# Router and step-size products with the thin weights stationary, in four column quarters of TensorE

## The reference

```python
g_prob = jax.nn.softmax((t @ w_rg + b_rg).astype(f32), axis=-1)      # 4 groups
e_logits = (t @ w_re + b_re).astype(f32).reshape(-1, N_GROUPS, EXPERTS_PER_GROUP)   # 16 experts
```

```python
dt = jax.nn.softplus((dt_raw + dt_bias).astype(jnp.float32))
log_f = jax.nn.log_sigmoid((f_raw + forget_b).astype(jnp.float32))
```

## Time and profile before

| | |
|---|---|
| median of 3 runs | 1540.35 us (1536.69 to 1540.72) |
| profiled execution | 1541.78 us, its span 1539.9 us |
| TensorE busy | 1384.1 us, 90% of the span |
| TensorE weight loads | 735.5 us, 48% |
| VectorE, ScalarE, GpSimd | 443.7, 240.1, 100.9 us |
| read from HBM | 355.14 MB, 231 GB/s over the span |
| mean granted clock of TensorE | 0.948 |
| L2045 (three routers), busy | 19.6 us, 96 passes |
| L2513 (step sizes), busy | 7.0 us, 32 passes |

### The profile page before, as it was taken

One profiled execution on the slowest core, in us unless ns is written; L12 is line 12 of the kernel. 1 busy time (PEld: TensorE's weight loads), 2 busy tenths in 40 slices (PEclk: granted clock), 3 DMA queues, 4 the chain that ended last, 5 costly groups with the idle time before them and its releaser, 6 DMA issues.

```text
span 1539.9 us, 18825 instructions
## 1 busy us (share of the span) xinstructions
PE 1384.1 (90%) x7765; PEld 735.5 (48%) x7765; DVE 443.7 (29%) x1252; ACT 240.1 (16%) x591; POOL 100.9 (7%) x190
## 2 busy tenths in 40 slices
PE   3999898999898888989997999979998699998996
PEld 3446554444445555554444874554455433333332
DVE  1104443221303355332214252251113721001113
ACT  0004210111101254101111222011320112010000
POOL 1110000000111000000001000000000011222210
PEclk9999989999998699989998899979999699999998
DMA  8957835999843356429999343365338147999990
GB/s 323 354 148 279 264 110 199 367 344 349 293 145 109 127 203 191 152 105 338 341 341 351 113 161 109 110 224 186 109 110 325 57 169 278 381 387 387 385 333 28
DMA packets 214687, 357.41 MB, mean 232 GB/s; under 512 B 15830, under 2 KB 85903, under 8 KB 214603
## 3 DMA queue, kind: packets, MB, share of 16 engines
q1 hardware_dynamic: 201314, 352.50, 64.6%
q10 hardware_dynamic: 13289, 3.71, 1.1%
HBM read 355.14 MB, written 1.05 MB: 231 GB/s over the span
## 4 chain that ended last, share of the span: by engine, by line
PE 82%; DVE 8%; DMA 4%; issue 3%; ACT 2%; SPq 1%; POOL 0%; DVEq 0%; ACTq 0%; POOLq 0%
PE bank L1924 19%; PE bank L2086 7%; PE bank L2284 6%; PE bank L2112 4%; PE bank L2127 4%; PE bank L2524 4%; PE bank L2144 4%; PE bank L2014 4%; PE bank L1939 3%; PE bank L2346 3%; DMA ring<-in_w_down 3%; PE bank L2571 3%; PE bank L2252 2%; PE bank L2377 2%; PE bank L2294 2%
## 5 line engine op out<-in xcount | busy, mean ns | idle before, releaser
L1924 PE MATMUL bank<-ring,hT 128*128 128x512 f32 x416 | 182.7, 601 | 3.2 <-ACT hT L804 3.0
L1924 PEld LDWEIGHTS bank<-ring,hT 128*128 128x128 f32 x416 | 79.9, 193 | 103.3 <-issue 99.9
L2086 PE MATMUL bank<-ring,A 128*64 128x512 f32 x512 | 113.4, 595 | 6.2 <-issue 3.2
L1924 PE MATMUL bank<-ring,OT 128*128 128x512 f32 x256 | 112.4, 600 | 3.0 <-issue 1.7
L1939 PE MATMUL bank<-ring,cact 128*32 128x128 f32 x2304 | 83.0, 298 | 24.5 <-DMA ring<-in_ada_w 14.7
L2284 PE MATMUL bank<-ring,A 128*64 128x512 f32 x384 | 86.9, 594 | 0.6 <-DMA ring<-in_w_up 0.6
L1939 PEld LDWEIGHTS bank<-ring,cact 128*32 128x32 f32 x2304 | 68.1, 119 | 36.8 <-issue 25.2
L682 POOL TENSOR_TENSOR rstd<-rstd,nhalf 128x1 f32<-128x1 f32 x20 | 17.2, 858 | 981.8 <-DVE rstd L1148 981.8
L1924 PEld LDWEIGHTS bank<-ring,OT 128*128 128x128 f32 x256 | 49.0, 193 | 64.2 <-issue 61.5
L2112 PE MATMUL bank<-pb 128*128 128x128 f32 (+1 forms) x512 | 64.4, 279 | 7.7 <-DVE A L1365 5.4
L2086 PEld LDWEIGHTS bank<-ring,A 128*64 128x64 f32 x512 | 36.2, 137 | 72.0 <-issue 68.7
(11 more groups left out here) (429 smaller groups left out, 1698.2 us busy)
## 6 DMA issues: line engine op xcount, KB each, us to landing
ring<-in_ada_w SPq DMA_DIRECT2D x24, 2048.0 KB, 8.7
ring<-in_moe_w_gate SPq DMA_DIRECT2D x32, 1024.0 KB, 7.2
ring<-in_moe_w_up SPq DMA_DIRECT2D x32, 1024.0 KB, 10.1
ring<-in_moe_w_down SPq DMA_DIRECT2D x16, 2048.0 KB, 12.9
ring<-in_w_gate SPq DMA_DIRECT2D x16, 2048.0 KB, 13.6
ring<-in_w_up SPq DMA_DIRECT2D x16, 2048.0 KB, 13.7
ring<-in_w_down SPq DMA_DIRECT2D x16, 2048.0 KB, 20.5
ring<-in_w_in SPq DMA_DIRECT2D x13, 2048.0 KB, 12.2
```

The costliest lines, as they stand in the source:

```text
L1924: ins = mm(B[2 * (m % 2) + tt][:], lhs[:, c, tt * P:(tt + 1) * P], w[:, c, :], start=c == 0, stop=c == C - 1)
L2086: ins = mm(B[4][n * b:n * (b + 1), :], h3[:, c, n * b:n * (b + 1)], wv[b][:, :, c, :], start=c == 0, stop=c == C - 1)
```

## The change

Three routers and the step-size product are computed the other way round. The thin weights (20 or 24 columns of a chunk) become the stationary operand and the 128 tokens of `hT` are streamed. Chunk c goes to the column quarter c % 4: its result of 20 or 24 rows stands at the partitions 32 * q of `B[2]`, and the eight chunks add up in pairs there. A product of zeros with 256 streamed columns clears the bank first. ScalarE copies the 128 x 256 of `B[2]` to `thin` in SBUF (`thin_copied`). Two products with that copy as stationary operand and a 128 x 24 matrix `fold` (ones where row 32 * q + j meets column j) add up the four quarters and turn the tokens back to the partitions, into the same place in `B[7]` or `B[6]` as before.

The order changes too. Token tile 0's products stand right behind `gate_spread` and ahead of tile 1's transposes; tile 1's, the copy and the fold stand where the router stood. For the step sizes both tiles' products stand where the old products did, and the fold comes after the first tile of `xbc`, with the signal for VectorE. GpSimd makes `fold` at the start with a memset and four selects. In two places on VectorE a wait for an own semaphore becomes `step`, a wait of the same kind.

The third MoE's work by halves of the experts is in the kernel before already; the diff holds nothing of it.

```diff
--- before.py
+++ after.py
@@ -247,6 +247,12 @@
         return ap.unsqueeze(axis).broadcast_to(shape)
 
 
+    fold = cols[:, 320:344]
+    thin = PT[:].rearrange("p a b -> p (a b)")[:, 0:T]
+    THIN = {"h1": 0, "h3": 1, "h4": 2, "h5": 3}
+
     def trans_evacuated(eng, k):
 
         eng.wait_ge(s["tr_act"] if k % 2 == 0 else s["tr_dve"], k // 2 + 1)
@@ -623,7 +629,11 @@
             pool.wait_ge(s["pool_step"], steps[0])
 
         g = nc.gpsimd
+        g.memset(fold, 0.0)
         step(g.memset(ident[:], 0.0))
+        for q in range(4):
+            step(g.affine_select(out=fold, in_=fold, compare_op=ALU.not_equal, fill=1.0, base=-32 * q,
+                                 pattern=[[-1, 24]], channel_multiplier=1))
         step(g.affine_select(out=ident[:], in_=ident[:], compare_op=ALU.not_equal, fill=1.0, base=0,
                              pattern=[[-1, P]], channel_multiplier=1))
         g.memset(zeros[:], 0.0)
@@ -774,6 +784,11 @@
                 if k % 2 == 0:
                     act.wait_ge(s["tr_ready"], k + 1)
                     op(k - TRANS[name], B[4]).then_inc(s["tr_act"], 1)
+
+        def thin_copied(hname):
+
+            act.wait_ge(s["thin_made"], THIN[hname] + 1)
+            a.copy(thin, B[2][:, 0:T]).then_inc(s["thin_out"], 1)
 
         def mod_out(G):
 
@@ -988,6 +1003,7 @@
         trans_out("h1", modulated(0, 3), [0])
         gate_rows(1)
         trans_out("h1", modulated(0, 3), [1])
+        thin_copied("h1")
         routing_exp(act, "moe0")
         moe_act("moe0")
         mod_out(3)
@@ -1022,10 +1038,12 @@
         act.wait_ge(s["proj_dve"], PROJ_DVE[PROJ["odout"] + 1])
         act.dma_start(rowp[:, 0, :], p["final_g"].partition_broadcast(P)).then_inc(s["rows_param"], 16)
         trans_out("h3", modulated(1, 3), [1])
+        thin_copied("h3")
         routing_exp(act, "moe1")
         moe_act("moe1")
         mod_out(6)
         trans_out("h4", modulated(2, 0))
+        thin_copied("h4")
 
         act.wait_ge(s["dt_abs"], 1)
         a.activation(dts[:, 1], dts[:, 1], ACT.Exp).then_inc(s["dt_exp"], 1)
@@ -1088,6 +1106,7 @@
         trans_out("h5", modulated(2, 3), [0])
         gate_rows(5)
         trans_out("h5", modulated(2, 3), [1])
+        thin_copied("h5")
         act.wait_ge(s["ln_scaled"], 1)
         routing_exp(act, "moe2")
         wide_act()
@@ -1346,9 +1365,8 @@
             step(v.tensor_tensor(rt[:, :, 4, :], rt[:, :, 4, :], rt[:, :, 7, 2:3].broadcast_to([P, TT, 4]), ALU.mult))
             step(v.tensor_tensor(rt[:, :, 5, :], rt[:, :, 5, :], rt[:, :, 7, 3:4].broadcast_to([P, TT, 4]), ALU.mult))
             step(v.tensor_tensor(rt[:, :, 4, :], rt[:, :, 4, :], rt[:, :, 5, :], ALU.add))
-            v.tensor_tensor(comb[:].rearrange("p t (g e) -> p t g e", g=4), bc(rt[:, :, 2, :], 3, [P, TT, 4, 4]),
-                            bc(rt[:, :, 4, :], 2, [P, TT, 4, 4]), ALU.mult).then_inc(s["comb_ready"], 1)
-            dve.wait_ge(s["comb_ready"], i + 1)
+            step(v.tensor_tensor(comb[:].rearrange("p t (g e) -> p t g e", g=4), bc(rt[:, :, 2, :], 3, [P, TT, 4, 4]),
+                                 bc(rt[:, :, 4, :], 2, [P, TT, 4, 4]), ALU.mult))
 
         def experts(name, gate):
             d = MOE[name]
@@ -1418,8 +1436,7 @@
                     step(v.tensor_tensor(tmp[:, h, :], B[2 * tt + h][:], gate[:, 512 * h:512 * (h + 1)], ALU.mult))
                     xs = x[:, tt, 512 * h:512 * (h + 1)]
                     ins = v.tensor_tensor(xs, xs, tmp[:, h, :], ALU.add)
-            ins.then_inc(s["moe_main"], 1)
-            dve.wait_ge(s["moe_main"], i + 1)
+            step(ins)
             moe_rest_dve(name, gate)
 
         def moe_rest_dve(name, gate):
@@ -2034,17 +2051,33 @@
 
             pe.wait_ge(s["max_ready"], max(it["soft"] + 1 for it in items if it["soft"] is not None))
 
-        def router(i, hname):
-
-            if i == 0:
-                pe.wait_ge(s["small_loads"], 16 * NSMALL)
-            for tt in range(TT):
+        def thin_products(w, n, hname, tts=(0, 1)):
+
+            if 0 in tts:
+                mm(B[2][:, 0:T], zeros[:], bc(ident[:], 1, [P, 2, P]), start=True, stop=True)
+            for tt in tts:
                 for g in range(2):
                     trans_evacuated(pe, TRANS[hname] + 2 * tt + g)
                 for c in range(C):
-                    ins = mm(B[7][:, 32 * tt:32 * tt + 20], hT[:, c, tt * P:(tt + 1) * P], wr[i][:, c, :],
-                             start=c == 0, stop=c == C - 1)
-            ins.then_inc(s["router_ready"], 1)
+                    q = c % 4
+                    ins = mm(B[2][32 * q:32 * q + n, tt * P:(tt + 1) * P], w[:, c, 0:n], hT[:, c, tt * P:(tt + 1) * P],
+                             start=False, stop=c >= 4, skip_group_check=True)
+            if 1 in tts:
+                ins.then_inc(s["thin_made"], 1)
+
+        def thin_folded(bank, n, hname):
+
+            pe.wait_ge(s["thin_out"], THIN[hname] + 1)
+            for tt in range(TT):
+                ins = mm(bank[:, 32 * tt:32 * tt + n], thin[:, tt * P:(tt + 1) * P], fold[:, 0:n], start=True, stop=True)
+            return ins
+
+        def router(i, hname):
+
+            if i == 0:
+                pe.wait_ge(s["small_loads"], 16 * NSMALL)
+            thin_products(wr[i], 20, hname, (1,))
+            thin_folded(B[7], 20, hname).then_inc(s["router_ready"], 1)
 
         def places(i):
 
@@ -2438,6 +2471,8 @@
         project("evout", 2, OT)
         token_transposes("h1", xn, "xn_ready", 2, tiles=[0])
         gate_spread(1)
+        pe.wait_ge(s["small_loads"], 16 * NSMALL)
+        thin_products(wr[0], 20, "h1", (0,))
         token_transposes("h1", xn, "xn_ready", 2, tiles=[1])
         pe.wait_ge(s["gate_rows"], 2)
         experts("moe0", "h1")
@@ -2500,6 +2535,7 @@
         project("odout", 2, OT)
         token_transposes("h3", xn, "xn_ready", 6, tiles=[0])
         gate_spread(3)
+        thin_products(wr[1], 20, "h3", (0,))
         token_transposes("h3", xn, "xn_ready", 6, tiles=[1])
         pe.wait_ge(s["gate_rows"], 4)
         experts("moe1", "h3")
@@ -2508,11 +2544,7 @@
         pe.wait_ge(s["moe_added"], 2)
         token_transposes("h4", xn, "xn_ready", 8)
         stage_transposed(pe, "h4")
-        for tt in range(TT):
-            for c in range(C):
-                ins = mm(B[6][:, 32 * tt:32 * tt + 24], hT[:, c, tt * P:(tt + 1) * P], wdf[:, c, :],
-                         start=c == 0, stop=c == C - 1)
-        ins.then_inc(s["dt_ready"], 1)
+        thin_products(wdf, 24, "h4")
 
         for j in range(4):
             m = PROJ["xbc"] + j
@@ -2524,6 +2556,8 @@
                     ins = mm(B[2 * (m % 2) + a // 2][:, (a % 2) * T:(a % 2 + 1) * T], w[:, c, a * P:(a + 1) * P],
                              hT[:, c, :], start=c == 0, stop=c == C - 1)
             ins.then_inc(tile_used, 1)
+            if j == 0:
+                thin_folded(B[6], 24, "h4").then_inc(s["dt_ready"], 1)
 
         pe.wait_ge(s["a_ready"], 1)
         for tt in range(TT):
@@ -2619,6 +2653,7 @@
         project("wo", 2, OT)
         token_transposes("h5", xn, "xn_ready", 10, tiles=[0])
         gate_spread(5)
+        thin_products(wr[2], 20, "h5", (0,))
         token_transposes("h5", xn, "xn_ready", 10, tiles=[1])
         pe.wait_ge(s["gate_rows"], 6)
         wide_experts()
```

6 lines of the change are left out of this document (3 added, 3 removed).

## The result

The new kernel takes 1516.2 us (median of 4 runs, 1514.33 to 1517.78) against 1538.52 for the kernel before, run beside it (4 runs, 1534.74 to 1540.72): ratio 0.987, 95% interval 0.984 to 0.990. A second comparison, made with the last experiments, gave 1520.68 (6 runs, 1515.52 to 1522.39) against 1534.66 (11 runs, 1526.36 to 1539.98): 0.990 (0.987 to 0.993), 14.0 us. So the gain is certain and its size is not known to better than some 4 us either way.

The account below looks back on a forecast made before the run. TensorE was taken to bound the kernel, with 82% of the chain ending last. Gains of 4.0 + 4.0 + 2.1 + 3.6 = 13.7 us, with 1.43 to the median, took 1541.78 to 1526.7 us; range 1519 to 1535.

Parts of the forecast that it names:

- The prices of the new form: Router and step-size products: 0.050 us a pass at 1.2 GHz, 0.026 at 2.4, plus ends; copy 0.37, fold 0.87 or 0.43.
- Rival 3: All changed stages: quarters don't run side by side, each pass takes 0.217 us; 8.3 us slower, 1548.7 us; chance 0.04.
- turning point: Time per quarter pass, about 0.14 us, at which the predicted gain turns into a loss.
- First and second MoE, 4.0 each: Routing in the first two MoEs: logits read earlier, gain 2.4 with the clock as before to 5.8 with it high.
- Rival 1: TensorE idles at `places` and the gathers, falls to 1.2 GHz, halving the gain; 6 us left, 1534 us; chance 0.14.
- Third MoE, 2.1: Routing in the third MoE: logits read earlier, gain 1.5 to 2.6 us, and all that follows moves with it.
- Step sizes, 3.6: Step-size stage (h4): product shortened from 6.8 to 2.8 us, fold 0.5 us behind first `xbc` tile; gain 2.5 to 6.1.
- rival 2: Loads set the pace, MoE gains are lost waiting for transfers; only the step sizes' 3.6 us stay, 1536.8 us; chance 0.07.
- the sum itself: Whole kernel: 4.0 + 4.0 + 2.1 + 3.6 = 13.7 us gained, bounds 8.8 and 20.3.
- Does the gain last?: Stages behind the MoE routing: loads start when TensorE frees a slot, so later transfers move along and the gain stays.

Follow-up runs that it names:

- E8: The new kernel with all eight chunks of a product in the first column quarter instead of four quarters; 1532.33 us.
- E9: The kernel before with ten useless 16-column products of zeros (20 pairs of weight load and product) at the start of TensorE's program; 1536.74 us.
- E10: The new kernel with 56 useless 16-column products of zeros (112 pairs of weight load and product) at the program's start; 1526.85 us.
- E13: The kernel before with 14 useless 16-column products of zeros (28 pairs of weight load and product) at the program's start; 1537.34 us.
- E5: The new kernel with one useless 512-column product of zeros behind the first `xbc` tile; 1523.67 us.
- E2: The kernel before with SyncE's and ScalarE's first loads held back at the start by four GpSimd memsets; 1538.09 us.
- E6: The kernel before with three useless 512-column products of zeros (2.56 us of work) behind the first `xbc` tile; 1539.72 us, ratio 1.001.
- E15: The new kernel, unchanged, measured a second time; 1520.68 us.

## Why the prediction was right in direction and wrong in size

**The prices of the new form** held: 0.04 us a pass at 2.4 GHz and 0.06 at 1.2 with the ends, for 0.68 and 1.25 us a tile forecast and 0.64 and 0.96 seen; copy 0.37; fold 0.52 to 0.62. The rows of L1939 were the right stand-in. Rival 3 fell (0.04 and not 0.217 us), and E8 tried its milder form: at 0.12 us a pass (0.19 at 1.2 GHz) the first and third routing are no faster than before, and the second and the step sizes are. That is near the turning point that was put at 0.14, and no test of it, since the whole also gains in stages that weren't changed.

**First and second MoE, 4.0 each.** First: 5.4 against the one trace of before, 3.9 against the usual 26.83 of the old routers (their median over six traces). Second: 1.9 or 5.4, by whether the clock falls ahead of the gathers. Rival 1's mechanism is real, but it acts in one place and in three traces of seven, and costs 3.5 us there.

**Third MoE, 2.1:** 2.25 measured.

**Step sizes, 3.6:** 5.56 measured, inside the bounds of 2.5 to 6.1. The term was mis-sized by leaving out what I had named: the clock rises with the first `xbc` tile and saves 2.3 us of it.

**Transfers** (rival 2) were no limit; all stages behind moved with the work.

**The step that failed** is the sum itself: it adds four places and takes everything behind them to move by the same time, with "Does the gain last?" asking only about loads. The runs show three things in its place. The code of TensorE was shifted, and a stop of 2.24 us in a group that nobody touched went away: E9, E10 and E13 take it away and bring it back. The clock at the end of the state-space part was low for 10.2 instead of 17.1 us, about 2.1 us, because the part begins at another instant: E5 undoes it with 0.85 us of nothing. And about 4.5 us of the profiled pair (3.0 ahead of h5, 1.5 ahead of h3) are not the change's: in the old code of E2, E6 and E9 the 3.0 are gone, and the 406 us between first inputs and h3 range over 6.4 us in all traces. E6, which up to `xbc` is the kernel before, has 411.3 there against 408.4, and 26.82 against 28.38 in the first routing; so an execution alone can move a stage by some 3 us, though E15 and E5 repeat the new kernel. The places together are then 3.9 + 1.9 to 5.4 + 2.25 + 5.56 = 13.6 to 17.1, with stop and clock 17.9 to 21.4, between the two measured gains of 14.0 and 22.3. The second gain is nearly the forecast's, and 1520.68 lies in its range; that is luck, since stop and clock gave their 4.3 us in E15's trace too. The narrow range was the second fault: it took in the bounds of the terms, and not what the clock alone does to a run.

What stays open: why the clock sometimes holds between `places` and the gathers, and what the 8.3 us between the two comparisons are made of. E15's trace has 2.4 us of them ahead of h1, where the clock was low for 13.6 us from 34 on; the others can't be seen in one trace a kernel.
